# Two decoder mixers on one core: modulation vectors turned, squares summed on GpSimd, rows and loads moved

## What is computed

```python
for l in range(2):
    shift1, scale1, gate1, shift2, scale2, gate2 = split(silu(c) @ w_ada[l] + b_ada[l], 6)
    h = x * (1 + scale1) + shift1
    y = hybrid_mixer(h, ...)
    x = layer_norm(ALPHA * x + gate1 * y, ...)
    h = x * (1 + scale2) + shift2
    f = swiglu(h) if l == 0 else top2_moe(h)        # 8 experts
    x = layer_norm(ALPHA * x + gate2 * f, ...)

def hybrid_mixer(h):
    z = h @ w_in       # c_q 256, c_kv 128, k_rope 64, gate_b 512, gate_c 512, u 512
    attn = causal attention of 4 heads from c_q, c_kv, k_rope
    conv = gate_b * causal_conv3(gate_c * u)
    y = concat(rms_norm(attn, g[:512]), rms_norm(conv, g[512:]))
    return y @ w_o
```

## Time and profile before

| | |
|---|---|
| runs of the kernel | 1432.64, 1434.14, 1434.12 us; median 1434.12 us |
| profiled execution | 1434.8 us, its span 1432.8 us |
| mean granted TensorE clock | 0.991 |
| busy | PE 98%, DVE 87%, ACT 70%, POOL 5% |
| input and mixer 0, to the first dense step | about 0 to 142 us |
| dense SwiGLU | about 142 to 342 us |
| mixer 1 | about 342 to 448 us |
| router | about 448 to 467 us |
| experts | about 467 to 1433 us |

### The profile page before, as it was taken

The page is one execution under the profiler, slowest core; times in us unless marked ns, Lnnn a source line. Parts: engine busy times, 40 slices in busy tenths (PEclk is TensorE's granted clock), DMA queues, the critical chain, the costliest instruction groups (busy, mean ns, idle before and its releaser), DMA issues.

```text
span 1432.8 us, 20275 instructions
## 1 busy us (share of the span) xinstructions
PE 1405.0 (98%) x7105; PEld 1162.9 (81%) x7105; DVE 1249.6 (87%) x1387; ACT 1006.4 (70%) x1241; POOL 65.4 (5%) x113
## 2 busy tenths in 40 slices
PE   6999999999999999999999999999999999999996
PEld 4785999997975888888888888888888888888885
DVE  5887788876787998998898999999889899999998
ACT  2443544445344888988888887888888888788884
POOL 1000000000000800000000000000000000002200
PEclk9999999999999999999999999999999999999998
DMA  9996398977565799999999999999999999999970
GB/s 363 404 356 231 124 376 294 361 273 281 205 233 204 287 389 366 382 385 369 373 398 367 373 387 391 366 382 382 371 372 398 366 371 389 390 367 381 413 312 32
DMA packets 203457, 482.18 MB, mean 337 GB/s; under 512 B 6928, under 2 KB 31614, under 8 KB 203402
## 3 DMA queue, kind: packets, MB, share of 16 engines
q1 hardware_dynamic: 198832, 470.31, 87.1%
q0 software_dynamic: 1584, 5.77, 1.0%
q10 hardware_dynamic: 2986, 5.38, 1.0%
HBM read 475.67 MB, written 5.77 MB: 336 GB/s over the span
## 4 chain that ended last, share of the span: by engine, by line
PE 95%; DVE 2%; DMA 2%; ACT 0%; issue 0%; POOL 0%; DVEq 0%; ACTq 0%; POOLq 0%
PE ps L1756 27%; PE ps L1758 27%; PE ps L1757 27%; PE ps L1917 2%; PE ps L1874 2%; PE ps L2105 2%; DMA raw<-in_w_ada_dram 1%; DVE ada_acc L1057 1%; PE ps L1934 1%; PE ps L1773 1%; PE ps L1725 1%; PE ps L1715 1%; PE ps L1825 0%; PE ps L2055 0%; DMA ada_bias<-in_b_ada_dram 0%; PE ps L1854 0%
## 5 line engine op out<-in xcount | busy, mean ns | idle before, releaser
L1393 DVE TENSOR_TENSOR low<-raw,w_hi 128x1024 fp32r<-128x1024 f32 x448 | 532.4, 1222 | 24.4 <-ACT w_hi L830 16.1
L830 ACT ACTIVATE w_hi<-raw 128x1024 fp32r<-128x1024 f32 x448 | 470.4, 1062 | 84.4 <-PE ps L1758 79.7
L1757 PE MATMUL ps<-low,h_hi 128*128 128x512 f32 x904 | 351.9, 389 | 0.0
L1756 PE MATMUL ps<-w_hi,h_lo 128*128 128x512 f32 x680 | 269.5, 396 | 0.0
L1758 PE MATMUL ps<-w_hi,h_hi 128*128 128x512 f32 x680 | 265.3, 390 | 0.0
L1757 PE MATMUL ps<-low,hid_hi 128*128 128x512 f32 x528 | 205.6, 389 | 0.0
L1757 PEld LDWEIGHTS ps<-low,h_hi 128*128 128x128 f32 x904 | 169.9, 188 | 34.1
L1393 DVE TENSOR_TENSOR low<-raw,e_hi 128x1024 fp32r<-128x1024 f32 x112 | 137.0, 1224 | 19.7 <-ACT e_hi L830 19.6
L1758 PEld LDWEIGHTS ps<-w_hi,h_hi 128*128 128x128 f32 x680 | 127.6, 188 | 27.4
L1756 PEld LDWEIGHTS ps<-w_hi,h_lo 128*128 128x128 f32 x680 | 127.8, 188 | 25.0
L1393 DVE TENSOR_TENSOR low<-raw,hx_lo 128x1024 fp32r<-128x1024 f32 x112 | 136.9, 1222 | 3.7
(11 more groups left out here) (377 smaller groups left out, 2288.7 us busy)
## 6 DMA issues: line engine op xcount, KB each, us to landing
raw<-in_moe_w_gate_dram SPq DMA_DIRECT2D x56, 2048.0 KB, 8.0
raw<-in_moe_w_up_dram SPq DMA_DIRECT2D x56, 2048.0 KB, 8.3
raw<-in_moe_w_down_dram SPq DMA_DIRECT2D x56, 2048.0 KB, 8.6
raw<-in_w_ada_dram SPq DMA_DIRECT2D x20, 2048.0 KB, 12.0
raw<-in_w_in_dram SPq DMA_DIRECT2D x6, 2048.0 KB, 16.1
raw<-in_ffn_w_gate_dram SPq DMA_DIRECT2D x11, 1024.0 KB, 7.4
raw<-in_ffn_w_up_dram SPq DMA_DIRECT2D x11, 1024.0 KB, 9.6
raw<-in_ffn_w_down_dram SPq DMA_DIRECT2D x11, 1024.0 KB, 5.9
```

What stands on the lines that cost most here:

```text
L830: act.activation(e_hi[k % ERING], raw[moe_slot(m)][:, (k % 4) * UNIT:(k % 4 + 1) * UNIT], ACT.Copy).then_inc(unit_hi, 1)
L1393: dve.tensor_tensor(low[moe_slot(m)][:, part], raw[moe_slot(m)][:, part], e_hi[k % ERING].bitcast(F32), ALU.subtract).then_inc(unit_lo, 1)
L1756: pe.matmul(o, x_lo, hi, start=first, stop=False, skip_group_check=True)
L1757: pe.matmul(o, x_hi, lo, start=False, stop=False, skip_group_check=True)
```

## The change

- `TURNED` gains vectors 3 and 4 of layer 0 and vector 4 of layer 1, so PE makes each with 4 + 4 transposes and ACT reads it with 4 + 4 accumulating copies. The second half of (0, 3) stands in PE's queue behind the scores of the first tile, and ACT's drain of it behind the convolution's squares. The halves of (0, 4) stand behind the two halves of the output rows of the first tile, those of (1, 4) before the query projection and behind it.
- Pool adds the four chunks of squares to one: for the convolution one add of 128x512 and one of 128x256, for the attention three of 128x256, of which the first needs only the first head pair. PE sums the one chunk left: 2 matmuls in place of 8. PE waits for Pool's semaphore in place of ACT's.
- Strip 4 is loaded ahead of `wc`.
- DVE's unit 4 comes ahead of the norm and rotary work, and the sums between the units are spread otherwise. In layer 0 `conv_part(0)` comes ahead of the attention's scaling; in layer 1 four late sums come ahead of it. `fold` comes behind the first tile's statistics. The low parts of the head stand later.
- The last gate is made between the router's two tiles, in place of two of three `warm` matmuls, and ACT's drains move there.

```diff
-BANK7 += [("ada", 0, 2, 0), ("ada", 0, 2, 1), ("ada", 0, 3, 0), ("ssq_conv", 0), ("ssq_attn", 0), ("ada", 0, 4, 0)]
+BANK7 += [("ada", 0, 2, 0), ("ada", 0, 2, 1), ("ada", 0, 3, 0), ("ada", 0, 3, 1), ("ssq_conv", 0), ("ssq_attn", 0), ("ada", 0, 4, 0), ("ada", 0, 4, 1)]
...
-TURNED = ((1, 0), (1, 1), (1, 3))
+TURNED = ((0, 3), (0, 4), (1, 0), (1, 1), (1, 3), (1, 4))
...
             load_pe(("wb", l), [(0, SLOT, KC, win_src(l, z0, z0 + D_CONV))], (mix_used, MIX_UNITS * l + 4))
+            if l == 0:
+                load_ada(0, 4)
             load_pe(("wc", l), [(0, SLOT, KC, win_src(l, z0 + D_CONV, z0 + 2 * D_CONV))], (mix_used, MIX_UNITS * l + 8))
-            for n in ((4,) if l == 0 else ()) + MIX_ADA[l][0]:
+            for n in MIX_ADA[l][0]:
...
+            for l in range(L):
+                pool.wait_ge(conv_sq, l + 1)
+                link(pool.tensor_tensor(sq[:, 0:2, :], sq[:, 0:2, :], sq[:, 2:4, :], ALU.add))
+                pool.tensor_tensor(sq[:, 0, :], sq[:, 0, :], sq[:, 1, :], ALU.add).then_inc(conv_folded, 1)
+                for b in range(2):
+                    pool.wait_ge(attn_sq, 2 * l + b + 1)
+                    ins = pool.tensor_tensor(sq[:, 2 * b, :], sq[:, 2 * b, :], sq[:, 2 * b + 1, :], ALU.add)
+                    link(ins)
+                pool.tensor_tensor(sq[:, 0, :], sq[:, 0, :], sq[:, 2, :], ALU.add).then_inc(attn_folded, 1)
...
                 act.wait_ge(conv_ready, l + 1)
                 act.activation(sq[:, :, :], cv[:, :, :], ACT.Square).then_inc(conv_sq, 1)
+                if l == 0:
+                    drain_ada(0, 3, 1)
...
                 if l == 0:
-                    drain_ada(0, 4)
+                    drain_ada(0, 4, 0)
+                    drain_ada(0, 4, 1)
                 else:
-                    drain_ada(1, 5, 0)
                     moe_hi(0, 0)
                     moe_hi(0, 1)
-                    drain_ada(1, 5, 1)
...
             layer_std(2, 1)
+            drain_ada(1, 5, 0)
             moe_hi(0, 5)
             modulate(3, 1, 2, None, 1)
+            drain_ada(1, 5, 1)
...
                 unit(3)
+                unit(4)
                 dve.wait_ge(rms_ready, l + 1)
...
-                sums(late, 2)
+                sums(late, 2 if l == 0 else 4)
+                if l == 0:
+                    conv_part(0)
...
-                fold(2 * l + 1)
                 behind(0)
                 layer_norm(2 * l, 0, gated)
+                fold(2 * l + 1)
                 normalise(2 * l, 0)
...
-                for k in ((0, 1), (2,), (), (3,))[part]:
+                for k in ((), (0,), (1, 2), (3,))[part]:
                     moe_lo(0, k)
...
                     m.then_inc(score_mm, 1)
+                    if l == 0 and t == 0:
+                        ada(0, 3, 1)
-
-                pe.wait_ge(conv_sq, l + 1)
+                pe.wait_ge(conv_folded, l + 1)
                 use_bank7(("ssq_conv", l))
                 for t in range(TT):
-                    for c in range(CC):
-                        m = pe.matmul(ps[:, 7, t:t + 1], sq[:, c, t * P:(t + 1) * P], ones[:, 0:1],
-                                      start=(c == 0), stop=(c == CC - 1))
+                    m = pe.matmul(ps[:, 7, t:t + 1], sq[:, 0, t * P:(t + 1) * P], ones[:, 0:1], start=True, stop=True)
...
                 if t == 1:
-                    warm(3, 1, 1)
+                    ada(1, 5, 0)
+                    warm(1, 1, 1)
+                    ada(1, 5, 1)
                     turn_input(3, 1)
```

More of the change, by code:

```diff
@@ L83 @@
 PE_ROWS = (1, 2, 3)
-BANK7 += [("ada", 0, 2, 0), ("ada", 0, 2, 1), ("ada", 0, 3, 0), ("ssq_conv", 0), ("ssq_attn", 0), ("ada", 0, 4, 0)]
+BANK7 += [("ada", 0, 2, 0), ("ada", 0, 2, 1), ("ada", 0, 3, 0), ("ada", 0, 3, 1), ("ssq_conv", 0), ("ssq_attn", 0), ("ada", 0, 4, 0), ("ada", 0, 4, 1)]
 BANK7 += [("ada", 0, 5, 0), ("ada", 0, 5, 1), ("ada", 1, 0, 0), ("ada", 1, 0, 1), ("ada", 1, 1, 0), ("ada", 1, 1, 1)]
-BANK7 += [("ada", 1, 2, 0), ("ada", 1, 2, 1), ("ada", 1, 3, 0), ("ada", 1, 3, 1), ("ada", 1, 4, 0)]
-TURNED = ((1, 0), (1, 1), (1, 3))
+BANK7 += [("ada", 1, 2, 0), ("ada", 1, 2, 1), ("ada", 1, 3, 0), ("ada", 1, 3, 1), ("ada", 1, 4, 0), ("ada", 1, 4, 1)]
+TURNED = ((0, 3), (0, 4), (1, 0), (1, 1), (1, 3), (1, 4))
 BANK7 += [("ssq_conv", 1), ("ssq_attn", 1), ("ada", 1, 5, 0), ("ada", 1, 5, 1)]
@@ L328, in trunk @@
         pt_mm, pt_ready = sem("pt_mm"), sem("pt_ready")
+        conv_folded, attn_folded = sem("conv_folded"), sem("attn_folded")
         conv_ready, conv_sq, conv_scaled = sem("conv_ready"), sem("conv_sq"), sem("conv_scaled")
@@ L625, in ada_init @@
                                                    ada_parts((k - 2) // VECS, (k - 2) % VECS) - 1)) + 1)
-                if (k // VECS, k % VECS) in TURNED and k % VECS == 1:
+                if (k // VECS, k % VECS) in TURNED and k % VECS in (1, 4):
                     act.activation(ada_acc[:, k % 2, :], ada_bias[:, :], ACT.Identity, scale=ident[:, k:k + 1],
@@ L638, in drain_ada @@
                 elif (l, vec) in TURNED:
-                    row = {0: 0, 1: 1, 3: 2}[vec]
+                    row = {0: 0, 1: 1, 3: 2, 4: 3}[vec]
                     for c in range(4):
@@ L763, in mixer @@
                 else:
-                    drain_ada(1, 4)
+                    drain_ada(1, 4, 0)
                 act.wait_ge(qn_mm, l + 1)
@@ L769, in mixer @@
                     drain_ada(0, 2, 1)
+                else:
+                    drain_ada(1, 4, 1)
                 act.wait_ge(kn_mm, l + 1)
@@ L775, in mixer @@
                 if l == 0:
-                    drain_ada(0, 3)
+                    drain_ada(0, 3, 0)
                 act.wait_ge(conv_ready, l + 1)
                 act.activation(sq[:, :, :], cv[:, :, :], ACT.Square).then_inc(conv_sq, 1)
+                if l == 0:
+                    drain_ada(0, 3, 1)
                 for t in range(TT):
@@ L1201, in mixer @@
                 if l == 0:
-                    sums(first, 1)
-                for n in range(4, MIX_UNITS):
+                    sums(first, 2)
+                for n in range(5, MIX_UNITS):
                     if n == 9:
-                        sums(first, 3 if l == 0 else 1)
+                        sums(first, 2 if l == 0 else 1)
                     unit(n)
-                    if l == 0 or n >= 9:
+                    if l == 0 and n == MIX_UNITS - 1:
+                        sums(first, 2)
+                    elif l == 0 or n >= 9:
                         sums(first, 1)
@@ L1288, in mixer @@
                 sums(late, len(late))
-                conv_part(0)
+                if l == 1:
+                    conv_part(0)
                 conv_part(1)
@@ L1810, in mixer @@
                 else:
-                    ada(1, 4)
+                    ada(1, 4, 0)
                 wait_load(pe, ("qkv", l))
@@ L1829, in mixer @@
                     ada(0, 2, 1)
+                else:
+                    ada(1, 4, 1)
                 for h in range(HEADS):
@@ L1844, in mixer @@
                 if l == 0:
-                    ada(0, 3)
+                    ada(0, 3, 0)
                 pe.wait_ge(qn_ready, l + 1)
@@ L1896, in mixer @@
                 conv_rows(1, 1, 6).then_inc(yc_mm, 1)
-                pe.wait_ge(attn_sq, 2 * (l + 1))
+                pe.wait_ge(attn_folded, l + 1)
                 use_bank7(("ssq_attn", l))
                 for t in range(TT):
-                    for c in range(HEADS):
-                        m = pe.matmul(ps[:, 7, t:t + 1], sq[:, c, t * P:(t + 1) * P], ones[:, 0:1],
-                                      start=(c == 0), stop=(c == HEADS - 1))
+                    m = pe.matmul(ps[:, 7, t:t + 1], sq[:, 0, t * P:(t + 1) * P], ones[:, 0:1], start=True, stop=True)
                 m.then_inc(bank7_full, 1)
-                if l == 1:
-                    ada(1, 5, 0)
                 pe.wait_ge(attn_scaled, l + 1)
@@ L1919, in mixer @@
                         m.then_inc(ya_mm, 1)
-                        if t == 0 and half == 0:
-                            if l == 0:
-                                ada(0, 4)
-                            else:
-                                ada(1, 5, 1)
+                        if t == 0 and l == 0:
+                            ada(0, 4, half)
             mixer(0)
```

## The result

| | before | after |
|---|---|---|
| runs | 1432.64 to 1434.14 us, median 1434.01 of 4 | 1421.06, 1421.45, 1423.45, 1425.21 us, median 1422.45 |
| ratio | | 0.9927, 95% interval 0.9915 to 0.9939 |
| profiled execution, its span | 1434.8, 1432.8 us | 1425.2, 1423.5 us |
| mean granted clock of that execution | 0.991 | 0.989 |

The ratio stands for 10.5 us gained; 15.95 were forecast. Measured twice more (E1 and E13), the changed kernel gave 0.9918 and 0.9912, so 11.7 and 12.6 us. The time is faster, as forecast, by two thirds to four fifths of the size. The four runs after lie over 4.2 us, and in each of them the mean clock is lower where the time is longer (0.993, 0.992, 0.991, 0.989). The four before lie over 1.5 us, but that was a short sample: the kernel before, measured beside E5, lay between 1430.60 and 1434.85 us, so a spread of 4 us is nothing that the change brought.

The account below looks back on a forecast made before the run. TensorE's own queue was taken to bound the kernel (95% of the chain). Terms of 4.65 + 2.5 + 5.1 + 1.7 + 2.0 = 15.95 us, taken from 1434.8 less 0.7, gave 1418.1 us, range 1414.5 to 1423.

Parts of the forecast that it names:

- (a): Rival at the folded squares: PE waits for Pool's adds, slowed beside DVE; 2.7 us lost, 1420.8 us; chance 0.17.
- (b): Rival at the start: reordering gives nothing, another wait holds PE and the clock still falls; 1422.8 us; chance 0.08.
- Term A: Start, blocks b and c: earlier strip 4 and unit 4 shorten PE's waits and avoid a clock fall; 4.65 us.
- Term B: Vectors 3 and 4 of layer 0, 4 of layer 1: transposes replace one-column rows on PE; 2.5 us.
- Term C: Four sums of squares in both layers: Pool folds them, PE runs 4 rows for 16, without waiting; 5.1 us.
- Terms D and E: Layer 1: gate matmuls leave the mixer, 1.7 us; the root's wait and the clock fall at 429.9 go, 2.0 us.
- Part 5: End of a mixer: DVE's reordering frees DVE, not PE, and is costed at nothing; PE's request comes 7.4 us earlier.
- The router: Behind the router's rows: the clock's fall may not come, 1.65 us, counted only in the range's lower end.

Follow-up runs that it names:

- E1: The changed kernel measured again, nothing edited: median 1420.48 us, ratio 0.9918 to the kernel before.
- E13: The changed kernel measured a third time, nothing edited: 1420.43 us, ratio 0.9912 to the kernel before.
- E5: The kernel before measured and profiled again, nothing edited: block b began at 49.09 us and block c ended at 72.72; no median of its own is given.
- E11: The changed kernel with one modulation sum before unit 5, two before unit 9 and three behind unit 11: 1421.55 us, ratio 0.9920 to the kernel before.
- E2: The kernel before with only the start changed (strip 4 loaded earlier, unit 4 earlier, sums spread): 1432.30 against 1432.41 us, ratio 0.9997.
- E12: The changed kernel with its start part undone (old load order, unit 4 and sums as before): 1422.78 us, ratio 0.9926 to the kernel before.
- E3: The changed kernel without Pool's additions, PE summing all four chunks of squares again: 1426.22 us, ratio 0.9957 to the kernel before.
- E4: The changed kernel with the last gate back in layer 1's mixer and three warming matmuls at the router: 1423.88 us, ratio 0.9945 to the kernel before.
- E6: The kernel before with four useless matmuls (3.44 us at full clock) ahead of block a in layer 0: median 1434.31 us, ratio 1.0013.
- E7: The changed kernel with four useless matmuls ahead of block a in layer 0: 1424.54 us, ratio 0.9948 to the kernel before.

## Why the prediction was right and wrong

The medians of the changed kernel (1422.45, 1420.48, 1420.43) lie inside the stated range of 1414.5 to 1423 and above the forecast of 1418.1. That is in part luck: the range reached so high only for rivals (a) and (b), and the times of both, 1420.8 and 1422.8, are near the mark, although Pool's waits cost 0.6 us and not 2.7 and (b)'s condition did not occur.

- **Term A, 4.65 us: the step that failed.** Its arithmetic held for the execution it was read from: 4.05 us measured, the new wait 1.07 us for 0.7, no fall near 61. (Its bound of 5.05 for no wait at all was low: the order of E11 has none and takes 28.72 - 23.39 = 5.33 us less.) The mistake was to take for the kernel. PE's arrival at unit 4 moves with the clock at the start, the release at 61.0 to 61.2 does not, and the profile of before showed the most idle time of three such executions of the old order. The reading of the windows had left out what would have warned: besides the three low stretches of the earlier trace rows, the profile of before has two ahead of block b, at 20.3 to 23.7 and 30.5 to 33.9 us, and it is their length that differs from one execution to the next. Over many executions the start alone gave 0.4 us by the ratio, with an error of 1.3 (E2); undoing it moved the median by 2.35, part of it behind the router (E12). Rival (b) named the outcome, "the start gives nothing", but for a reason that did not occur (another wait in its place and the fall all the same); the wait was simply not always there.
- **Term B, 2.5 us: right.** With the other parts taken off: 25.08 - 23.82 = 1.26, 42.96 - 42.64 (E3) = 0.32, and 60.82 - 59.91 = 0.91, together 2.49. ACT held PE 0.19 us for the second part of vector 3 (its start at 99.75 against a gapless 99.56), where 0.1 was allowed. These are differences between stages; the turned vectors were not undone by themselves.
- **Term C, 5.1 us: too high by 0.6.** 4.47 by E3. I took no wait for Pool; PE waits in layer 0 about 0.15 and 0.09 us (its starts at 103.85 and 122.16 against a gapless 103.70 and 122.07), and 0.32 in layer 1 before the attention's sum. The additions took 1.27 and 0.73 us where they met no large DVE instruction (1.2 and 0.6 estimated), and one in each fold met one. Rival (a) had the mechanism right and its size wrong, 0.6 us for 2.7: one addition per fold was lengthened, not every one.
- **Terms D and E.** The gate's 1.7 and the root's 0.35 are there: 2.23 by E4, less the 0.2 that the gate costs at the router, where I took nothing. The 1.65 us for the clock at 430 were a draw, like those at 61: E2, E5 and E6, with the old rows, show no fall there, and E4 shows none with the wait back. Taking a fall seen in one execution as a price of the code was the same mistake as in term A.
- **Part 5, nothing: right.** DVE holds PE nowhere between the sum of squares and the router. (The 7.4 us by which PE was to come earlier there should have read 7.1 by the part's own terms.)
- **The router, where I allowed a gain of 1.65 us,** turned the other way in the profiled execution (14.43 for 12.83) and the allowed way in E1 and E13 (11.64 and 11.62). The three are the same program.
- Free of any low clock, the change is worth 2.49 + 4.47 + 2.23 - 0.17 = 9.0 us behind the start, against 9.65 forecast for these (2.5 + 5.1 + 1.7 + 0.35). The 6.3 us that were forecast on top (4.65 and 1.65) gave 1.5 to 3.6 by the three ratios, each with an error of 1.7 to 2.1.

What stays open: why the clock was low behind the router's rows in E12 and not in E13 (13.10 and 11.62 us), and whether moving the whole program by a microsecond, or the gate among the router's rows, changes how often it falls there. Sixteen profiles show that it differs; they don't show a rule. How often the old order meets each of the rows of the last table isn't known either, so the start's worth over many executions is known no better than by E2's 0.4 us with its error of 1.3 and E12's 2.35.

## What to carry to other kernels

An idle wait whose release is set by a DMA, behind a stretch of PE whose clock varies, is a buffer: the release stays and the idle time shrinks when PE is late, until the release depends on PE again (E6). Removing it gains the idle time only in executions where it stands, so ask what moves the arrival and what the release, and look at a second profile of the old kernel before pricing it. A fall of the clock in one trace is a price of that execution until a second one shows it. And compare stages between rows, execution against execution with equal clocks: here that gave terms B and C and the gate to about 0.1 us, where the medians of the changed kernel lie 2 us apart.

## What the runs showed of the hardware

- The same rows at the start were granted half clock for 6.8, 10.2 or 13.7 us in all before block b, in different executions of equal code; block b then began at 45.6 to 46.0, 47.5 to 48.2, or 48.8 to 49.3 us. (E6 and E7, with work added there, came later.) Behind the router's rows it was 0, 3.4 or 6.8 us. Before each fall PE had run one-column or eight-column rows or had stood idle; the same rows were also run without a fall.
- Pool beside DVE: an addition of 256 elements took 0.73 us, and 1.72 beside a modulation sum, which has two large SBUF inputs:

```profile
100.73 1.27 POOL L569 TENSOR_TENSOR h_t<-h_t 128x512 f32<-128x512 f32 x1 [96.12 <-ACT h_t L794]
102.07 1.72 POOL L570 TENSOR_TENSOR h_t<-h_t 128x256 f32<-128x256 f32 x1
```
```profile
101.94 1.27 DVE L1075 SCALAR_TENSOR_TENSOR ada_acc<-raw,c_act,ada_acc 128x1024 f32<-128x1024 f32 x1
```

The addition ends 0.58 us after the DVE instruction that it met; the 8-element row ended 0.06 us after its own. So the price is about what is left of that instruction. It is paid once and is not a slower rate: the next addition of this kind ends 0.58 us after the sum that it met (120.25 to 121.53) as well, although the second sum ran beside it from 121.56 on.

```profile
120.37 1.73 POOL L575 TENSOR_TENSOR h_t<-h_t 128x256 f32<-128x256 f32 x1
```
```profile
120.25 2.94 DVE L1075 SCALAR_TENSOR_TENSOR ada_acc<-raw,c_act,ada_acc 128x1024 f32<-128x1024 f32 x2
```

- DVE pays too: these two sums took 2.94 us, and 2.60 in E3, where Pool does nothing. Here nobody waited for them.

```profile
118.07 2.60 DVE L1065 SCALAR_TENSOR_TENSOR ada_acc<-raw,c_act,ada_acc 128x1024 f32<-128x1024 f32 x2
```

The Trainium skill ("GPSIMD Engine Reference", Key points) names the contention, and the trace agrees with 0.73 against 1.72 us. By the rate that the same page of the Trainium skill gives for such an add (section "Elementwise — side-by-side cycle accounting") 256 elements were an estimate of 0.55 us; the measured 0.73 decides.
